# Second MLP matrices of three chunks by Strassen's scheme in a two-layer fp32 kernel

## What is computed

```python
# first layer
h2 = rmsnorm(x, norm_mlp_g[layer])
x = x + jnp.square(jax.nn.relu(h2 @ w_mlp_in[layer])) @ w_mlp_out[layer]
# second layer
def squared_relu_mlp(u, w_ff1, w_ff2):
    hdn = jnp.square(jax.nn.relu(jnp.einsum('bld,df->blf', u, w_ff1)))
    return jnp.einsum('blf,fd->bld', hdn, w_ff2)
h = h + squared_relu_mlp(rmsnorm_2(h, norm_ffn[l]), w_ff1[l], w_ff2[l])
```

## Time and profile before

| | |
|---|---|
| median of 3 runs | 1447.32 us (1446.65 to 1447.49) |
| the profiled execution | 1447.7 us, span 1446.0 us |
| TensorE matmul busy | 1438.4 us, 99% |
| TensorE weight load busy | 1160.5 us, 80% |
| DVE, ACT, Pool busy | 772.9, 496.1, 69.8 us |
| granted TensorE clock, mean | 1.000 |

### The profile page before, as it was taken

One profiled execution on the slowest core, in us unless ns is written; L12 is line 12 of the kernel. 1 busy time (PEld: TensorE's weight loads), 2 busy tenths in 40 slices (PEclk: granted clock), 3 DMA queues, 4 the chain that ended last, 5 costly groups with the idle time before them and its releaser, 6 DMA issues.

```text
span 1446.0 us, 18666 instructions
## 1 busy us (share of the span) xinstructions
PE 1438.4 (99%) x7710; PEld 1160.5 (80%) x7710; DVE 772.9 (53%) x978; ACT 496.1 (34%) x702; POOL 69.8 (5%) x98
## 2 busy tenths in 40 slices
PE   9999999999999999999999999999999999999998
PEld 7887778677888888888878997778888888888886
DVE  5535433766665354453556678655756445353551
ACT  4125532654433122222243435343443222122232
POOL 4000000000110000000022020000020000000000
PEclk9999999999999999999999999999999999999999
DMA  5233122111233322322323222232223222323311
GB/s 178 90 105 91 59 88 88 59 59 55 92 94 100 99 87 94 109 87 87 101 77 100 88 67 74 88 103 88 87 87 110 95 87 87 106 97 116 131 58 59
DMA packets 125525, 131.10 MB, mean 91 GB/s; under 512 B 2330, under 2 KB 122500, under 8 KB 125460
## 3 DMA queue, kind: packets, MB, share of 16 engines
q1 hardware_dynamic: 125444, 130.16, 27.9%
q10 hardware_dynamic: 16, 0.00, 0.0%
HBM read 127.28 MB, written 2.10 MB: 89 GB/s over the span
## 4 chain that ended last, share of the span: by engine, by line
PE 98%; DVE 1%; ACT 1%; issue 0%; POOL 0%; POOLq 0%; DVEq 0%
PE ps L1807 82%; PE ps L1803 4%; PE ps L1871 3%; PE ps L2100 1%; PE ps L2127 1%; PE ps L2113 1%; PE ps L2216 1%; DVE wl L1201 0%; PE ps L1919 0%; PE ps L2004 0%; PE ps L1980 0%; PE ps L1911 0%; PE ps L2045 0%; PE ps L2024 0%; PE ps L1896 0%; PE ps L2298 0%
## 5 line engine op out<-in xcount | busy, mean ns | idle before, releaser
L1807 PE MATMUL ps<-Ah,wh 128*128 128x512 f32 x992 | 394.7, 398 | 0.4
L1807 PE MATMUL ps<-Al,wh 128*128 128x512 f32 x992 | 392.3, 395 | 0.0
L1807 PE MATMUL ps<-Ah,wl 128*128 128x512 f32 x992 | 390.5, 394 | 0.0
L1807 PE MATMUL ps<-Bh,wh 128*128 128x512 f32 x736 | 291.4, 396 | 0.2 <-issue 0.2
L1807 PE MATMUL ps<-Bl,wh 128*128 128x512 f32 x736 | 291.2, 396 | 0.0
L1807 PE MATMUL ps<-Bh,wl 128*128 128x512 f32 x736 | 289.5, 393 | 0.0
L1807 PEld LDWEIGHTS ps<-Ah,wh 128*128 128x128 f32 x992 | 186.4, 188 | 47.1 <-DVE wl L1201 2.0
L1807 PEld LDWEIGHTS ps<-Ah,wl 128*128 128x128 f32 x992 | 186.7, 188 | 42.4
L1807 PEld LDWEIGHTS ps<-Al,wh 128*128 128x128 f32 x992 | 186.3, 188 | 41.9 <-issue 0.5
L765 ACT ACTIVATE wh<-raw 128x1024 fp32r<-128x1024 f32 x110 | 116.4, 1058 | 277.9 <-PE ps L1807 277.9
L714 ACT ACTIVATE wh<-raw 128x1024 fp32r<-128x1024 f32 (+2 forms) x135 | 126.7, 938 | 227.3 <-PE ps L1807 216.3
(11 more groups left out here) (282 smaller groups left out, 1201.9 us busy)
## 6 DMA issues: line engine op xcount, KB each, us to landing
raw<-in_w_in SPq DMA_DIRECT2D x38, 1024.0 KB, 5.4
raw<-in_w_ff SPq DMA_DIRECT2D x29, 1024.0 KB, 5.3
raw<-in_w_mlp_in SPq DMA_DIRECT2D x16, 1024.0 KB, 5.3
raw<-in_w_mlp_out SPq DMA_DIRECT2D x16, 1024.0 KB, 5.2
raw<-in_w_out SPq DMA_DIRECT2D x8, 1024.0 KB, 5.2
late<-in_w_ff SPq DMA_DIRECT2D x3, 1024.0 KB, 5.3
arena<-in_x SPq DMA_DIRECT2D x4, 512.0 KB, 6.8
raw<-in_w_up_sb SPq DMA_DIRECT2D x2, 1024.0 KB, 5.0
```

The source lines that it names most:

```text
L1807: last = pe.matmul(dense_psum(t_ps, kind), a[:, k, :], b[:, o0 + k, col0:col0 + S1], start=start, stop=stop)
```

## The change

In the three loop chunks of both MLPs the second matrix is multiplied by Strassen's scheme in Winograd's form. A pair of slabs (two blocks of output features), the two halves of the contraction (4 blocks each) and the two halves of the tokens (256 columns each) make a 2 x 2 by 2 x 2 block product, done with seven block products instead of eight: A11·B11, A12·B21, S1·T1, S2·T2, S3·T3, S4·B22 and A22·T4. Each has 4 k by 3 matmuls of 256 columns. The parts:

- the hidden blocks are kept in seven forms of 256 tokens (B11, T1, T2, T3, T4, B21, B22; high in the tensor `AA` or `BB`, low in `Hl`). For hidden blocks 0 to 3 DVE makes one difference per slab, for blocks 4 to 7 (slabs 4 to 7) two in one operation, and Pool a third (`t4_diff`); ACT and DVE split them;
- the weight sums S1 = A21 + A22 and S3 = A11 - A21 are made by Pool (`s13_sums`), S2 = S1 - A11 and S4 = A12 - S2 by DVE (`own_sums`), and all are split by ACT and DVE; these preparations for pair q+1 stand between the PSUM readings of pair q;
- products that several output quarters share go by way of `mids`, to which DVE adds two banks at a time over all chunks; Pool adds `mids` to `X` once, when a loop is over;
- four PSUM banks per pair, two sets in turn; the fifth product (S4·B22) accumulates into a bank from which DVE must first have read (`mid_read`);
- relu squared is now one DVE operation from PSUM (max with 0, times the scale) and a Square on ACT;
- the new buffers (`Hl`, `Sh`, `Sl`, `zf`) share memory with `W2h`, `W2l` and `late`, and the places of the W2 conversions in the last chunk move.

The core of the diff:

```diff
+        with ExitStack() as inner:
+            Hl = inner.enter_context(nc.sbuf_tensor("Hl", [P, 4, 7 * HB], F32R))
+            Sh = inner.enter_context(nc.sbuf_tensor("Sh", [P, 3 * S1], F32R))
+            Sl = inner.enter_context(nc.sbuf_tensor("Sl", [P, 3 * S1], F32R))
+            zf = inner.enter_context(nc.sbuf_tensor("zf", [P, 2048 + 2048 + 3072 + 1280], F32))
...
-        W2_AT = (0, 1, 4, 5, 6, 7)
+        W2_AT = (2, 3, 5, 6, 7)
+        W2_AT_OUT = {0: 5, 2: 6, 3: 7}
...
+        mids = zf[:, 0:2048].rearrange("p (q n) -> p q n", q=4)
+        sums = zf[:, 2048:4096].rearrange("p (s n) -> p s n", s=4)
+        first_half = zf[:, 4096:7168].rearrange("p (k b n) -> p k b n", k=4, b=3)
+        second_half = zf[:, 7168:8448].rearrange("p (b n) -> p b n", b=5)
...
+        def pair_banks(q):
+
+            base = 4 * (q % 2)
+            return base + 2, base, base + 3, base + 1
...
+            def strassen_sums(which):
+                t0, _, p0 = MLPS[which]
+                pool.memset(mids, 0.0).then_inc(mids_zero, 1)
+                if which == REAL:
+                    add_squares(3, REAL)
+                with pool.Fori(0, CHUNKS - 1) as c:
+                    for q in range(4):
+                        if q == 0:
+                            fourth_difference(which, c, 4)
+                        s13_sums(which, c, q)
+                        if q == 0:
+                            for j in range(5, 8):
+                                fourth_difference(which, c, j)
...
+                x = X[:, :, META:S2].rearrange("p (q o) (t n) -> p q o t n", o=2, t=2)
+                n = 4 if which == REAL else 0
+                pool.tensor_tensor(x[:, :, 0, 1], x[:, :, 0, 1], mids[:, :, 0:HB], ALU.add).then_inc(x_combined, 1)
+                pool.tensor_tensor(x[:, :, 1, 0], x[:, :, 1, 0], mids[:, :, 0:HB], ALU.add).then_inc(x_combined, 1)
...
+            def s13_sums(which, c, q):
+                p0 = MLPS[which][2]
+                p, u = p0 + 4 + q, so_far(which, 4) + 4 * c + q
+                pool.wait_ge(w_landed[p % 2], landed_count(p0, 4 + q) + 64 * c)
+                if q > 0:
+                    pool.wait_ge(s1_lo, u)
+                pool.tensor_tensor(blk(sums[:, 0]), quarter(p, 1, 0), quarter(p, 1, 1), ALU.add).then_inc(s1_sum, 1)
+                if q > 0:
+                    pool.wait_ge(s34_lo, u)
+                pool.tensor_tensor(blk(sums[:, 2]), quarter(p, 0, 0), quarter(p, 1, 0), ALU.subtract)\
+                    .then_inc(s3_sum, 1)
+
+            def fourth_difference(which, c, j):
+                pool.wait_ge(t_diff, so_far(which, 8) + 8 * c + j + 1)
+                pool.tensor_tensor(second_half[:, 2], second_half[:, 3], second_half[:, 0], ALU.subtract)\
+                    .then_inc(t4_diff, 1)
+
...
+                for j in range(8):
+                    k = j % 4
+                    f = first_half[:, k, 0:3:2] if j < 4 else second_half[:, 3:5]
+                    if j < 6:
+                        act.wait_ge(slab_done, t + j + 1)
+                        slab_weights(j + 2)
+                    if j == 6:
+                        second_sum(0)
+                    act.wait_ge(evac_done, t + j + 1)
...
+                                       ACT.Copy).then_inc(hid_hi, 1)
+                    else:
+                        act.activation(hidden_part(Hh, k, T2_, 2), second_half[:, 0:2].rearrange("p b n -> p (b n)"),
+                                       ACT.Copy).then_inc(hid_hi, 1)
+                        act.wait_ge(t4_diff, fourths + k + 1)
+                        act.activation(hidden_part(Hh, k, T4, 3), second_half[:, 2:5].rearrange("p b n -> p (b n)"),
+                                       ACT.Copy).then_inc(hid_hi, 1)
...
+                for q in range(4):
+                    done = blocks + 6 * q
+                    if q < 3:
+                        act.wait_ge(blk_done, done + 1)
+                        upper_left(q + 1)
+                        act.wait_ge(blk_done, done + 2)
+                        first_sum(q + 1)
+                        act.wait_ge(blk_done, done + 3)
+                        second_sum(q + 1)
+                        act.wait_ge(blk_done, done + 5)
+                        last_sums(q + 1)
+                        act.wait_ge(slab_done, t + 8 + 2 * q + 2)
...
+                def own_sums(q):
+                    p = p0 + 4 + q
+                    if q > 0:
+                        dve.wait_ge(s2_lo, pairs + q)
+                        dve.wait_ge(s34_lo, pairs + q)
+                    dve.wait_ge(s1_sum, pairs + q + 1)
+                    dve.tensor_tensor(blk(sums[:, 1]), blk(sums[:, 0]), quarter(p, 0, 0), ALU.subtract)\
+                       .then_inc(s2_sum, 1)
+                    dve.wait_ge(s2_sum, pairs + q + 1)
+                    dve.tensor_tensor(blk(sums[:, 3]), quarter(p, 0, 1), blk(sums[:, 1]), ALU.subtract)\
+                       .then_inc(s4_sum, 1)
+
...
+                for j in range(8):
+                    k = j % 4
+                    f = first_half[:, k, 0:3:2] if j < 4 else second_half[:, 3:5]
+                    dve.wait_ge(slab_done, t + j + 1)
+                    if j >= 5:
+                        dve.wait_ge(hid_lo, parts + 4 + 2 * k)
+                    dve.scalar_tensor_tensor(out=f, in0=halves(dense_psum(t0 + j, which)), scalar=0.0,
+                                             in1=halves(RS[:, 0:S1]), op0=ALU.max, op1=ALU.mult).then_inc(evac_done, 1)
+                    if j < 6:
+                        slab_weights(p0 + (j + 2) // 2, j % 2, t + j + 3)
+                    if j == 6:
+                        second_sum(0)
+                    if j == 7:
+                        last_sums(0)
+                    dve.wait_ge(hid_sq, squares + j + 1)
+                    if j < 4:
+                        h = first_half[:, k]
+                        dve.tensor_tensor(h[:, 1], h[:, 2], h[:, 0], ALU.subtract).then_inc(t_diff, 1)
+                        dve.wait_ge(hid_hi, parts + j + 1)
+                        dve.tensor_tensor(hidden_part(Hl, k, B11, 2), h[:, 0:2].rearrange("p b n -> p (b n)"),
+                                          hidden_part(Hh, k, B11, 2), ALU.subtract).then_inc(hid_lo, 1)
+                    else:
+                        h = second_half
+                        dve.tensor_tensor(h[:, 0:2], h[:, 4:5].to_broadcast([P, 2, HB]), first_half[:, k, 1:3],
+                                          ALU.subtract).then_inc(t_diff, 1)
+                        dve.wait_ge(hid_hi, parts + 4 + 2 * k + 1)
+                        dve.tensor_tensor(hidden_part(Hl, k, T2_, 2), h[:, 0:2].rearrange("p b n -> p (b n)"),
+                                          hidden_part(Hh, k, T2_, 2), ALU.subtract).then_inc(hid_lo, 1)
+                        dve.wait_ge(hid_hi, parts + 4 + 2 * k + 2)
+                        dve.tensor_tensor(hidden_part(Hl, k, T4, 3), h[:, 2:5].rearrange("p b n -> p (b n)"),
+                                          hidden_part(Hh, k, T4, 3), ALU.subtract).then_inc(hid_lo, 1)
+                    if j == 5:
+                        own_sums(0)
+                    if j == 6:
+                        upper_left(0)
+                        first_sum(0)
+                    if j == 7:
+                        lower(0)
+
+                for q in range(4):
+                    g1, g2, g3, g4 = pair_banks(q)
+                    done, last = blocks + 6 * q, q == 3
+                    x0, x1 = X[:, 2 * q, META:S2], X[:, 2 * q + 1, META:META + HB]
+                    mid = halves(mids[:, q])
+                    dve.wait_ge(blk_done, done + 2)
+                    dve.tensor_tensor(mid, mid, ps[:, g1:g3 + 1, 0:HB], ALU.add).then_inc(mid_read, 1)
+                    if not last:
+                        own_sums(q + 1)
+                    dve.wait_ge(blk_done, done + 4)
+                    dve.wait_ge(mid_read, reads + 2 * q + 1)
+                    dve.tensor_tensor(mid, mid, ps[:, g2:g4 + 1, 0:HB], ALU.add).then_inc(mid_read, 1)
+                    if last:
+                        slab_weights(p0, 0, t + 17)
+                    else:
+                        upper_left(q + 1)
+                        first_sum(q + 1)
+                    dve.wait_ge(blk_done, done + 6)
+                    dve.tensor_tensor(halves(x0), halves(x0), ps[:, g1:g3 + 1, 0:HB], ALU.add)
+                    if not last:
+                        second_sum(q + 1)
+                        last_sums(q + 1)
+                    dve.wait_ge(slab_done, t + 8 + 2 * q + 2)
+                    dve.tensor_tensor(x1, x1, ps[:, g4, 0:HB], ALU.add).then_inc(evac_done, 2)
+                    if last:
+                        slab_weights(p0, 1, t + 18)
+                    else:
+                        lower(q + 1)
...
+                        if m == 0:
+                            dve.wait_ge(x_combined, 4)
...
+                        if g in W2_AT_OUT:
```

(65 more changed lines are left out.)

259 lines of the change are left out of this document (173 added, 86 removed).

## The result

The changed kernel takes **1460.24 us** (median of 4 runs, 1459.51 to 1460.88) against 1447.26 for the kernel before beside it: a ratio of 1.009, 95% interval 1.0073 to 1.0108. It is slower by 13.0 us, where 5.0 were forecast. The direction held and the whole range of 1438 to 1466 did; the size did not, and the time lies above the 1447 to 1458 that the forecast proper was given.

A forecast was written before the change was run, and what follows sets the result against it. The prediction took TensorE, busy 99% at full clock, to bound the kernel. Matmul savings of 27.6 us, first-pair waits of 29.8 and a 2.8 tail summed to +5.0: 1452.7 us profiled, 1452.3 by the median, range 1438 to 1466.

The forecast's parts named there:

- the forecast proper: The case that the whole kernel comes as forecast, with a range of its own of 1447 to 1458 us; chance 0.47.
- TensorE's own work: Second matrices: 336 matmuls of 256 columns at 118.7 ns replace 192 of 512, saving 4.60 us a chunk, 27.6 for six.
- The rival of a short pitch: All second matrices: 256-column matmuls are quicker than 118.7 ns; at 110 ns the kernel takes 1437.7 us; chance 0.15.
- The first pair: After slab 4, DVE's queue delays S4·B22 from 22.39 to 27.36 us; TensorE stands 4.97 us a chunk, 29.8 for six.
- The four times behind a Pool sum: DVE's splits of slabs 4 and 7 stand behind Pool's sums for pairs 0 and 1, 3.28 us a chunk.
- The answers of ACT: In DVE's first-pair queue, four round trips to ACT between difference and split, 4 x 0.79 = 3.16 us a chunk.
- Three pieces of wait: TensorE's first-pair waits: about 2.0 us before A11·B11, 1.2 at the last k of S2·T2, 1.7 before S4·B22.
- Pairs 1 to 3 keep up: In pairs 1 to 3 DVE needs at most 9.71 us against TensorE's 9.97, so it keeps up by 0.26.
- The tail: Before output block 4, TensorE waits once for W2's part 7, converted behind block 3: 2.8 us.
- The queue is longer: First pair: DVE operations 0.06 dearer, Pool's sums at 1.34 us, or both; 1458 to 1471, about 1464; chance 0.25.
- DVE and Pool cost each other nothing: First pair: Pool's sums fall where DVE waits anyway, 2.1 us less a chunk, 12.8 in all, 1440; chance 0.09.
- the waits all hide: All the scheme's waits hide and only the wait before output block 4 stays, giving 1423 us; chance 0.04.

The follow-up runs named there:

- the edit made for it: The changed kernel with W2's last three parts converted at output blocks 0, 1 and 2 instead of 0, 2 and 3: 1457.65 us.
- the fillers: The changed kernel with 16 useless 256-column matmuls before TensorE's first-pair wait for A11's low part and 12 before that for mid_read: 1456.34 us.
- the fastest: The changed kernel with DVE's first-pair reordering, W2's last parts one output block earlier, and DVE's waits for ACT filled by later operations: 1432.79 us.
- the last one above: The 1432.79 us kernel with Pool's pair-1 sums held until pair 0's lower half is split, and DVE's pair-1 A11 split before the two sums: 1443.38 us.
- DVE's order, without and with W2: The changed kernel with pair 0's lower-half split behind the first PSUM read, pair 1's sums behind the second: 1444.97 us; plus W2's last parts one block earlier: 1441.05.
- Pool held back alone: The changed kernel with Pool's two pair-1 sums waiting until DVE has split the lower half of pair 0: 1454.21 us.

## Why the prediction was right in kind and short in size

- **TensorE's own work** (118.7 ns a matmul, 4.60 us a chunk saved): 119.0, and 4.5. Right. The rival of a short pitch falls.
- **The first pair** (S4·B22 at 27.36 us behind slab 4's end, 4.97 us of waits): 27.8 and 5.3. Right in mechanism, with two terms that miss in opposite directions. The four times behind a Pool sum had 3.28 us; the operations in question are 0.67 and 0.31 us longer at slab 4 (1.63 and 1.53 instead of 0.96 and 1.22) and 0.67 and 1.06 at slab 7, 2.7 in all. The answers of ACT had 4 x 0.79 and a share of 0.94 for shorter gaps; in fact each slab has a second wait of 0.34 us, for the high part of T4, and with the overlap lost at both the four slabs lose 4 x 1.20 = 4.8 to ACT, before any self-wait. Pool's sum, taken at 1.04 us, is 1.29 where Pool is alone (486.66 us of the trace), near the 1.34 that I kept as a bound; it is how long Pool holds that counts.
- **Three pieces of wait** (2.0, 1.2, 1.7): 2.19, 0.18, 2.90. The sum nearly holds, the split doesn't: the wait for the last k of S2·T2 nearly vanished into that for the read.
- **Pairs 1 to 3 keep up:** they do, in one stream of 288 matmuls.
- **The tail** (2.8 us): 2.67, and it went with the edit made for it.
- **The step that failed** is the sentence the clock stands in: I read nines in every slice and carried full clock into a kernel that waits. No term was put for it. Each chunk has a slow stretch, three of six in the open, 1.56 us each, 4.7 in the trace and 3.9 by the fillers. The spans differ by 12.1 us, 7.1 more than the sum, and the clock is 4.7 of them. Of the rest 1.8 us are the first pair's 0.30 a chunk, and 0.6 the matmul's 119.0 for 118.7 ns.
- **Rivals.** "The queue is longer" had 1458 to 1471 and the result lies in that interval, but by its reason only in part, so that the range held by luck as much as by working: it reached up to 1466 for this rival, and what filled it was mostly the clock, which no rival had. Pool at 1.3 was so, dearer DVE operations were not (0.68 to 0.69 each, as in the earlier trace rows). "DVE and Pool cost each other nothing" falls by the run without sums (priced at 2.1 us a chunk, it gave 2.2); "the waits all hide" would have needed an order of DVE that the change didn't have.

What stays open: about 1 us of the 13.0 that the medians show beyond the bill by the trace (11.9), of which some 0.4 is that the profiled execution of the kernel before was that much above its median. Open is also what decides where the clock falls. In the profiled execution with W2 one block earlier four of the six slow stretches lie in the open, in that of after three, and the edit touches neither place; so single differences of 1 to 2 us between kernels can be the clock's place alone.

## What to carry to other kernels

When an operation is taken off the engine that bounds a kernel and ten are put on a helper, lay the helper's queue out to the first operand that is needed, and ask of each operation in front whether it must stand there: a single split out of place cost 2 us a chunk here, nearly half of what the scheme saved on TensorE, and moving it, with the slow stretches of the clock that went with it, turned 0.9% slower into 0.2% faster. Two engines that exclude each other are one queue, and what hides in the idle time of one comes out when that time is filled. Price each new wait of TensorE with the clock behind it.

## What the runs showed of the hardware

**DVE and Pool exclude each other operation by operation, and in these rows only where DVE's operation has both inputs in SBUF.** First chunk of the changed kernel, in pair 1, DVE and Pool:

```profile
479.01 1.99 DVE L1399 TENSOR_TENSOR wl<-raw,wh 128x1024 fp32r<-128x1024 f32 x1
480.92 0.68 DVE L1450 TENSOR_TENSOR zf<-zf,ps 128x512 f32<-128x512 f32 x1
481.52 1.17 DVE L1373 TENSOR_TENSOR zf<-zf,raw 128x512 f32<-128x512 f32 x1
```
```profile
478.07 1.84 POOL L719 TENSOR_TENSOR zf<-raw 128x512 f32<-128x512 f32 x1 [6.59 <-DMA raw<-in_w_mlp_out]
479.86 2.28 POOL L722 TENSOR_TENSOR zf<-raw 128x512 f32<-128x512 f32 x1
```

The sum at 479.86 holds up to 482.14. Inside it the addition at L1450, with one input in PSUM, runs at its own 0.68 us; the next, with both inputs in SBUF, takes 1.17. The Trainium skill, VectorE: DVE Perf Modes, section "Two Vector instructions with no wait between them", has an operation with two tensor inputs in SBUF read its second one through an interface shared with GpSimd; the rows agree, and show what it costs: each waits out what is left of the other's.

**The clock can fall behind a wait of 2 to 3 us in a stream that is otherwise full,** for some 3.4 us, to 0.50. How often it did so, in the profiled executions:

- in none of the chunks whose waits were at most 1.55 us (the kernel without Pool's sums, the fastest, the last one above);
- in two and in three of six chunks behind 2.19 with a second wait of 0.7 (DVE's order, without and with W2), in five of six behind 2.19 with a second of up to 1.31 (Pool held back alone);
- in every chunk behind 2.19 with a second wait of up to 2.90, and behind 2.79;
- behind the tail's wait of 2.7 in two of six kernels that have it.

The Trainium skill, TensorE: Matmul & The Clock Gate, Part 1, puts the clock down to how busy the array has been of late. The run with fillers agrees for the waits that it fills: work without use keeps the clock there.
